# A fused encoder layer on one core: adaLN pieces by contraction tile, the output projection's end by column blocks, gate rows in pass 0

## What is computed

```
mod = c @ ada_w + ada_b                       # 2048 -> 6*2048
sh1, sc1, gt1, sh2, sc2, gt2 = split(mod, 6)
h = modulate(rmsnorm(x, norm1_g), sh1, sc1)
u = h @ w_in                                  # branches and gate pre-activations
merged = sum over 4 branches of sigmoid(gate) * y
x = x + gt1 * (merged @ w_o)                  # x1
h2 = modulate(rmsnorm(x, norm2_g), sh2, sc2)
# router: top group of 4, then the top 2 of 8 experts in it
x = x + gt2 * hier_moe(h2, ...)               # 32 SwiGLU experts, width 512
return rmsnorm(x, final_g)
```

## Time and profile before

| | us |
|---|---|
| median of 3 runs | 1788.24 |
| lowest and highest run | 1787.34, 1788.6 |
| profiled execution, span from first to last instruction | 1788.8 |

### The profile page before, as it was taken

One profiled execution on the slowest core, in us unless ns is written; L12 is line 12 of the kernel. 1 busy time (PEld: TensorE's weight loads), 2 busy tenths in 40 slices (PEclk: granted clock), 3 DMA queues, 4 the chain that ended last, 5 costly groups with the idle time before them and its releaser, 6 DMA issues.

```text
span 1788.8 us, 25899 instructions
## 1 busy us (share of the span) xinstructions
PE 1740.1 (97%) x10197; PEld 992.0 (55%) x10198; DVE 898.3 (50%) x1041; ACT 389.4 (22%) x472; POOL 0.8 (0%) x5
## 2 busy tenths in 40 slices
PE   4999999999999999999999999999999999999997
PEld 3888567777777776875444444444444444444432
DVE  5564968867778678566232323233333333333334
ACT  3001034333333333443111101010101010101011
POOL 0000000000000000000000000000000000000000
PEclk9999999999999999999999999999999999999999
DMA  9998538889879697646999999999999999999996
GB/s 370 387 374 327 188 142 336 330 312 353 332 287 363 250 373 306 227 164 246 422 422 422 422 422 422 422 421 422 421 422 422 422 422 422 422 421 422 422 422 253
DMA packets 137455, 641.95 MB, mean 359 GB/s; under 512 B 9027, under 2 KB 9155, under 8 KB 77123
## 3 DMA queue, kind: packets, MB, share of 16 engines
q1 hardware_dynamic: 136978, 639.18, 89.4%
q0 software_dynamic: 144, 1.70, 0.2%
q10 hardware_dynamic: 290, 0.46, 0.1%
HBM read 639.21 MB, written 2.10 MB: 359 GB/s over the span
## 4 chain that ended last, share of the span: by engine, by line
PE 75%; DMA 21%; DVE 2%; SPq 1%; issue 1%; ACT 0%; DVEq 0%
DMA ring<-in_exp_w 18%; PE ps L920 18%; PE ps L884 7%; PE ps L675 7%; PE ps L677 7%; PE ps L676 7%; PE ps L580 6%; PE ps L637 5%; PE ps L907 4%; PE ps L862 3%; PE ps L593 3%; DMA ring<-in_ada_w 2%; PE ps L748 2%; PE ps L749 2%; PE ps L750 2%; DVE r_m L1322 1%
## 5 line engine op out<-in xcount | busy, mean ns | idle before, releaser
L920 PE MATMUL ps<-ring 128*64 128x512 f32 x2048 | 466.7, 598 | 5.7 <-DMA ring<-in_exp_w 5.7
L920 PEld LDWEIGHTS ps<-ring 128*64 128x64 f32 x2048 | 143.4, 137 | 293.3 <-issue 293.2
L1690 DVE TENSOR_TENSOR r_h<-r_h,ps 128x1024 f32<-128x1024 f32 x124 | 145.9, 1218 | 205.2 <-PE ps L907 205.2
L676 PE MATMUL ps<-g_lo,h_hi 128*128 128x512 f32 x512 | 199.3, 389 | 0.0
L1663 DVE TENSOR_TENSOR r_c<-ps,scale 128x512 f32<-128x512 f32 x64 | 44.0, 687 | 283.9 <-PE ps L862 280.8
L1234 ACT ACTIVATE r_m<-ps 128x512 f32<-128x512 f32 x32 | 19.1, 597 | 699.3 <-PE ps L920 699.3
L675 PE MATMUL ps<-mix_hi,h_hi 128*128 128x512 f32 x384 | 156.6, 408 | 0.0
L1107 ACT ACTIVATE mix_hi<-ring 128x1024 fp32r<-128x1024 f32 x96 | 101.5, 1061 | 222.4 <-PE ps L677 222.4
L677 PE MATMUL ps<-mix_hi,h_lo 128*128 128x512 f32 x384 | 149.7, 390 | 0.0
L580 PE MATMUL ps<-r_h,ring 128*128 128x256 f32 x640 | 142.3, 385 | 1.3 <-ACT r_h L1058 1.3
L1414 DVE SCALAR_TENSOR_TENSOR r_m<-ring,col,r_m 128x2048 f32<-128x2048 f32 x53 | 124.3, 2346 | 31.4 <-DMA ring<-in_ada_w 31.4
(11 more groups left out here) (270 smaller groups left out, 1619.2 us busy)
## 6 DMA issues: line engine op xcount, KB each, us to landing
ring<-in_exp_w SPq DMA_DIRECT2D x320, 1024.0 KB, 20.2
ring<-in_ada_w SPq DMA_DIRECT2D x78, 1024.0 KB, 8.2
ring<-in_w_in SPq DMA_DIRECT2D x36, 2048.0 KB, 10.0
r_b<-in_exp_w SPq DMA_DIRECT2D x64, 1024.0 KB, 22.2
ring<-in_w_in SPq DMA_DIRECT2D x20, 1024.0 KB, 14.2
r_b<-in_ada_w SPq DMA_DIRECT2D x18, 1024.0 KB, 9.7
ring<-in_w_o SPq DMA_DIRECT2D x8, 2048.0 KB, 9.6
ring<-in_branch_w SPq DMA_DIRECT2D x6, 2048.0 KB, 8.4
```

What stands on the lines that cost most here:

```text
L676: mm(ps[:, b + t, :], h, lo[:, cols], start=False, stop=False)
L920: last = mm(ps[m * NWIN:(m + 1) * NWIN, 2, :], xe[:, k, :], chunk(2 * c + m)[:, kk * F:(kk + 1) * F], start=(k == 0), stop=(k == KT - 1))
L1690: V.tensor_tensor(x1n, x1n, ps[:, (6, 4)[b]:(6, 4)[b] + 2, :].rearrange("p b n -> p (b n)"), ALU.add).then_inc(added, 1)
```

## The change

Three places are touched.

1. In the head, the last piece of each part is loaded as four transfers of 512 KB, one for each contraction tile with shift and scale together, each with a semaphore of its own, and VectorE waits for each tile. The two saves of part 0 (units 3 and 4) go from VectorE to ScalarE.
2. At the end of the output projection the loops are turned: column block n outside, token half t inside. Pieces 30 and 29 change places on ScalarE and VectorE, so that the columns of blocks 0 and 1 need pieces 28 and 30 alone. x1, transposes, copies and logits also go by n, then t. Transposed blocks of t = 0 are copied by VectorE, those of t = 1 by ScalarE. The reciprocals of both roots are one instruction; the diagonals `root_diag` are made by ScalarE.
3. The matmuls for the gt2 rows leave the stretch between the first gathers and stand in pass 0 behind the first quarter of `first`; ScalarE saves the rows there.

```diff
+                if piece == 3:
+                    for kk in range(4):
+                        sp.dma_start(head_ada(i)[:, kk, :, :],
+                                     ada_v[:, 12 + kk, 0:2 * D].rearrange("p (v n) -> p v n", v=2)
+                                     [:, :, part * PART:(part + 1) * PART]).then_inc(ada_last[kk], 16)
+                    return
...
-            pe.wait_ge(g_lo_done, 128 + 32)
-            for t in range(TT):
-                for n in range(4):
+            for n in range(4):
+                pe.wait_ge(g_lo_done, 128 + (30 if n < 2 else 32))
+                for t in range(TT):
                     for k in (14, 15):
                         last = wo_products(k, t, n)
                     last.then_inc(wo_done, 1)
...
+            for n in range(4):
+                for t in range(TT):
+                    turn_x1(n, t)
+                if n == 1:
+                    pe.wait_ge(rw_scaled, 1)
+                if n:
+                    for t in range(TT):
+                        logit_part(n - 1, t)
...
+                    if not with_second and c == 0:
+                        gate2_row()
...
+                if k == 3:
+                    for n in (3, 4):
+                        act.wait_ge(head_used, used(0, n))
+                        A(late[:, n - 3, :], ps[:, 6:8, :].rearrange("p b n -> p (b n)"), ACT.Copy
+                          ).then_inc(part_added, 1)
...
-            for y in range(AHEAD + 1, 32):
+            for y in (*range(AHEAD + 1, 29), 30, 29, 31):
                 wo_high(y)
...
             A(stat[:, 20:21], keep[:, K_EPS:K_EPS + 1], ACT.Sqrt).then_inc(warm_up, 1)
+            copy_turned(0)
             square(0, 0)
+            copy_turned(1)
+            square(1, 0)
+            copy_turned(2)
             square(0, 1)
             root(0)
-            square(1, 0)
-            part_high(0)
+            copy_turned(3)
             square(1, 1)
             root(1)
+            part_high(0)
             part_high(1)
...
+            for n in range(4):
+                save_x1(n, 0)
+                if n:
+                    save_turned(n - 1)
+                save_x1(n, 1)
+            save_turned(3)
```

More of the change, by code:

```diff
@@ L178, in used, with ada_count @@
             return HEAD * part + ORDER[part].index(n) + 1
+        def ada_count(i):
+            return 32 * sum(j % ADA_FIRST == i % ADA_FIRST and j % 4 != 3 for j in range(i + 1))
         def head_w(i):
@@ L213, in build @@
         ada_in = [sem(f"ada_in{i}") for i in range(ADA_FIRST)]
+        ada_last = [sem(f"ada_last{i}") for i in range(4)]
         part_added = sem("part_added")
@@ L784, in _, with turn_x1, logit_part @@
                     last.then_inc(wo_done, 1)
-            for m in range(8):
-                t, n = m // 4, m % 4
-                pe.wait_ge(x1_ready, m + 1)
+            def turn_x1(n, t):
+                pe.wait_ge(x1_ready, 2 * n + t + 1)
                 for k in range(4):
-                    last = nc.tensor.transpose(ps[:, m, k * P:(k + 1) * P],
+                    last = nc.tensor.transpose(ps[:, 4 * t + n, k * P:(k + 1) * P],
                                                x1_k[:, t, n, k, :], ident)
                 last.then_inc(x1_turned, 1)
[L795 to L801, removed]
+            def logit_part(n, t):
+                pe.wait_ge((x1T_ready, x1T_copied)[t], n + 1)
                 for k in range(4 * n, 4 * n + 4):
                     side = k % 2
-                    last = mm(ps[side * NWIN:(side + 1) * NWIN, t, 0:P], rws[:, k, :], x1T[:, k, t * P:(t + 1) * P],
+                    last = mm(ps[side * NWIN:(side + 1) * NWIN, 4 * t, 0:P], rws[:, k, :], x1T[:, k, t * P:(t + 1) * P],
                               start=(k < 2), stop=(k >= KT - 2))
@@ L807, in _ @@
                     last.then_inc(logitT_done, 1)
+            for n in range(4):
[6 more added lines that the diff above has]
+                        logit_part(n - 1, t)
+            mm(ps[:, 5, 0:36], ones, cst_k[:, :], start=True, stop=False)
+            mm(ps[:, 5, 0:36], ones[0:1, :], lrow[0:1, :], start=False, stop=True).then_inc(cst_done, 1)
+            for t in range(TT):
+                logit_part(3, t)
             def logits(t):
@@ L909, in combine, with gate2_row @@
                 last.then_inc(comb_done, 1)
+            def gate2_row():
+                pe.wait_ge(diag2_ready, 1)
+                for b in range(2):
+                    for side in range(2):
+                        o = 4 * (2 * b + side)
+                        last = mm(ps[side * NWIN:(side + 1) * NWIN, 6 + b, :], ones[:, 0:NWIN], diag2[:, o:o + 4, :],
+                                  start=True, stop=True)
+                last.then_inc(gt2_row, 1)
             def first(p, with_second, last_pass=False):
@@ L957, in _ @@
             gather_parts((0, 1))
[L958 to L965, removed]
             pe.wait_ge(lo_ready, 8)
@@ L1525, in _ @@
                             mod[:, GT2, :].unsqueeze(2).broadcast_to([P, KT, P]), ALU.mult).then_inc(diag2_ready, 1)
-            for y in range(24, 32):
+            for y in (*range(24, 29), 30, 29, 31):
                 wo_low(y)
             step(V.tensor_scalar(minus, ident, -1.0, None, ALU.mult))
[L1530 to L1534, removed]
@@ L1536, in _ @@
             v.wait_ge(x_again, 16)
             v.wait_ge(row_saved, 2)
[L1538 to L1552, removed]
+            def save_x1(n, t):
+                v.wait_ge(wo_done, 2 * n + t + 1)
+                prod = slot(5)[:, t * MIX:(t + 1) * MIX]
+                step(V.tensor_tensor(prod, ps[:, 4 * t + n, :], gt1row[:, n * MIX:(n + 1) * MIX], ALU.mult))
+                x1n = x1[:, t, n * MIX:(n + 1) * MIX]
+                V.tensor_tensor(x1n, x1n, prod, ALU.add).then_inc(x1_ready, 1)
```

58 lines of the change are left out of this document (34 added, 24 removed).

## The result

| | before | after |
|---|---|---|
| median, us | 1787.47 (20 runs) | 1789.91 (20 runs) |
| lowest, highest | 1785.42, 1789.99 | 1787.29, 1793.67 |

The ratio is 1.0015, its 95% interval 1.0009 to 1.0021: the change costs 2.4 us (1.6 to 3.8). The forecast was a gain of 1.0. The profiled execution after has a time of 1790.77 and a span of 1789.0. A run's time lies 1.8 above its span, so the span of before, 1788.8, belongs to a run of some 1790.6, 3.1 above the median of its kernel and above the highest of its twenty runs. The two profiled spans are 0.2 apart where the medians are 2.4 apart, and the first thing to find is why.

What follows compares the result with a forecast made beforehand. The prediction took the expert-weight stream, started by TensorE's first release, as the bound, with TensorE ahead of it. Terms −1.4 − 0.65 + 0 + 0.75 + 0.3 = −1.0 us gave 1787.2 us, 8-in-10 range 1785.0 to 1790.2.

Steps and rivals of the forecast that it cites:

- −0.2 up to the gather: Router to first gather: later remainders (+1.7) and removed gt2 rows (−1.9) sum to −0.2 us, taken as 0.
- −1.4: Head: copy leaves VectorE's chain in part 1, a small wait leaves part 0; 1.4 us gained.
- −0.65: Head, behind part 1's sums: shorter quiet stretch, even chance that the clock stays up; half of 1.3 us gained.
- +1.7: Start of the remainders: ScalarE's scaled copy begins only behind roots, reciprocal and a diagonal; 1.7 us later.
- +0.75: Between last logits and remainders: quiet 2.5 us, even chance of a clock fall costing 1.5 us.
- −1.9: First gathers: gt2 rows fall out of TensorE's work there, 1.9 us of issue saved.
- +0.3: Pass 0: gt2 rows free later weight chunks 1.9 us later, nearly all covered by slack; 0.3 us lost.
- The 4.1 us: Projection's end: last product 4.1 us earlier without the idling and half clock, given back at once by VectorE's wait.
- The end moves as S moves: Expert-weight stream: never stops after S, its first load issue at 836.65 us; the remaining 952.15 us are its own.
- no slack in the stream: Rival, pass 0: gt2 rows cost the stream their full 1.9 us, giving 1788.8 us; chance 0.12.
- faster: Rival, projection's end: the 4.1 us reach the stream, giving 1783.1 us; chance 0.08.
- the 1.2 GHz through all remainders: Slower rival: TensorE's clock falls and stays low up to the first gather, +7.5 us, 1794.0 us; chance 0.06.

Runs made afterwards that it cites:

- e1: Head part of the change alone (last adaLN piece by contraction tile, part 0 saves on ScalarE), against the kernel before: 1785.95 us, ratio 0.9994.
- e4: Head and projection parts together, gt2 rows left between the first gathers, against the kernel before: 1789.32 us, ratio 1.0013.
- e3: Only the gt2 rows moved out of the gathers into pass 0, against the kernel before: 1787.87 us, ratio 1.0008.
- e2: Projection part alone (x1, transposes and logits by column blocks), gt2 rows left between the gathers, against the kernel before: 1792.31 us, ratio 1.0027.
- e12: e11 plus two unused matmuls in the head, ahead of and behind the sums of part 0: 1784.41 us, ratio to before 0.9983.
- e11: e10 plus two unused 256-column matmuls in TensorE's wait ahead of pass 0's first gather: 1785.01 us, ratio to before 0.9985.
- e7: Changed kernel with each pair of x1 blocks transposed behind the products of the next column block: 1787.07 us, ratio to before 0.9999.
- e8: e4 plus seven unused matmuls in TensorE's wait ahead of the remainders, mis-sized at 6.22 us: 1793.48 us, ratio to before 1.0037.
- e5: Changed kernel with the high bf16 parts made in blocks of 512 columns: 1789.26 us, ratio to before 1.0014.
- e6: Changed kernel with the gt2 rows moved from pass 0 into TensorE's wait ahead of the remainders: 1787.92 us, ratio to before 1.0007.
- e10: e7 and e6 together, early transposes and gt2 rows ahead of the remainders: 1785.27 us, ratio to before 0.9992.
- e9: e7 and e5 together, early transposes and high parts in blocks: 1785.63 us, ratio to before 0.9993.

## Why the prediction was wrong, by its steps

The runs give each part of the change a price, to be held against the terms of the prediction (which add up to −1.2 here, since the prediction took its −0.2 up to the gather as 0):

| part | forecast, us | runs, us |
|---|---|---|
| head: e1 less before | −1.4 − 0.65 = −2.05 | −1.2 |
| projection's end to the remainders, with the clock there: e4 less e1 | +1.7 + 0.75 = +2.45 | +3.4 |
| gt2 rows: after less e4 | −1.9 + 0.3 = −1.6 | +0.6 |
| sum | −1.2 | +2.8 |

After and e4 ran on different chips, so their difference is rough. Still the gt2 rows hold the largest miss: a gain was forecast and none came. e3, the rows alone, has +0.75 (interval −0.2 to +3.0), which excludes −1.6.

**1. Head, −1.4 and −0.65: too large, read from one execution.** Copy and wait are gone in after. But the wait of 1.67 us and the fall behind it belong to the one execution that was read, not to the kernel. e2 and e3 have the head of before, with the copy. TensorE lost more to a fall of the clock in part 0 there (0.62 and 0.66 granted from 36 to 45 us, against 0.81 in before), asked later, and waited 0.41 us and not at all; e3:

```profile
74.00 1.95 PE L554 MATMUL ps<-keep,r_m 128*128 128x1 f32 x16
...
76.00:80.00 4.00, 4.00 (x20) 3.51 (x20) 0.33 (x2) 2.07 (x4) 0.00 (x0) 1.00 1.06 387
```

So the clock stayed up behind part 1 without the edit, and e12, with it, has half clock there. The sums of part 2 begin at 110.46 and 110.43 in e2 and e3, and at 109.66 to 110.01 in the eight executions of e4 to e11, which have the new head and a like clock in part 0: 0.4 to 0.8 us is what the edit gave. After and e1 fell further in part 0 (0.53) and stand at 111.44 and 111.34. So the head of before's execution was some 1.8 late, as far as these two tell, and that of after some 1.4 late against the eight, which nearly cancels. That the edit gains is likely (e1 −1.2, with an interval that holds zero; e4 3.0 below e2, whose intervals meet); its size is open. Nor does every microsecond of the head arrive: of the 0.9 by which e1's sums come earlier than those of before, 0.6 is left at the projection's end. The prediction had no term for the fall in part 0.

**2. Projection's end: right in mechanism.** The 4.1 us came, and VectorE's 4.80 us of waiting gave them back; with e7's order 3.3 of them arrive at the remainders. Relative to the last logits the remainders come 1.8 later (forecast 1.7), and the router is 0.2 late, together the +2.0 of e2. The balance of −0.2 up to the gather was not reached, since with the gt2 rows out TensorE waits 0.45 us there for VectorE.

**The clock, +0.75: half of its price, and in another place.** A coin between 0 and 1.5 was taken, for the wait ahead of the remainders. Of the profiled executions with this wait of 1.71, e2, e4 and e7 had the fall behind it and after had not (granted 1.00 from 813.21 to 826.50). That, and not the rows of 1.92 and 2.56 us, which are of two lengths, shows the same stretch falling on either side. The fall is worth 1.65 in e4 against e8. After fell at the gathers instead, where the dense gt2 rows had stood, and this was not priced at all: its sixteen matmuls took 5.02 us for 3.5, and from `first` to S lie 5.21 us against 4.18 before, so 1.0 reached S. That this is near the 0.75 is luck. The clock fell at the gathers in after, e5, e6 and e10, and not in e3, e7 and e9, which lack the rows too; with rows (before, e1, e2, e4, e8) or filler (e11, e12) it never did. That the rows held it is thus likely, and not shown. The Trainium skill, page "TensorE: Matmul & The Clock Gate", section "HAM oscillation — how this bites in real kernels", tells of a kernel in which waits between bursts of matmuls bring the array back to its slow clock, so that the next burst starts slow. The rows of after and of e10 agree in kind, behind waits of about 0.45 us.

**3. gt2 rows in pass 0, +0.3: the step that failed.** "The end moves as S moves" took S as the release that binds, and the slack was worked out for the second and third pair alone. The fifth pair is released by TensorE too, behind the gt2 rows, the rest of pass 0 and the first quarter of pass 1. Before, it was issued 3.6 us ahead of its need; 3.0 later, with a stream that had begun 1.1 later and lost 0.5, it had 2.2, too little by 1.3. That this pair bound is shown for this execution. How much later than S the stream ends, against before, tells what the rows cost it:

| execution | later behind S, us |
|---|---|
| rows in pass 0: after, e3, e5, e7, e9 | **+1.4**, **+1.7**, +0.3, +0.7, +0.5 |
| rows elsewhere: e1, e2, e4, e6, e8, e10, e11, e12 | 0.0, +0.1, +0.1, −0.1, 0.0, −0.3, 0.0, −0.5 |

The two groups do not meet: the rows in pass 0 cost the stream something each time. How much varies, and why is open. In after, e5, e7 and e9 a hole stands some 22 us behind S, at the fifth pair; e3 loses its share ahead of that. The rival "no slack in the stream" had 1.9. So most of the −1.9 in step 2 was no gain: rows taken out of the gathers and put ahead of the later releases still delay these. The latency was too kind as well: 1.6 us from issue to bytes, taken from a start; what a stream that runs dry needs is more. The windows of after have 57 GB/s from 0.3 to 1.3 us behind the issue at 837.72, half the rate up to 2.3 us, and full rate only from there on. The Trainium skill, page "DMA: Bandwidth & Descriptors", section "Specifications", gives about 0.6 us to the first byte for loads issued by SP; the first of these windows agrees, and of the time to full rate, which decides here, the figure says nothing.

Put together from the two profiled executions: −0.8 at the sums of part 2, +0.8 from there to `first`, +1.0 from `first` to S, +1.4 behind S, +2.5 in all (rounded terms). These add up by construction, and each is of one execution. Of the rivals "no slack" came true in good part; "faster" was there to be had only with another order of TensorE's list and the rows elsewhere (e11); the 1.2 GHz through all remainders did not come.

Two slips are in the prediction's frame. The median was taken as 0.6 below the execution that was read; time against time it lies 2.4 below, and the median of twenty runs 3.1. And the terms named for the upper end of the range give 1788.24 + 0.4 + 0.5 + 1.6 = 1790.7, not 1790.2. Neither moves the forecast.

Open: how often each fall of the clock happens. The profiles show one execution each. The median of e2 (+5.2, against 3.4 for e4 less e1) may hold more of them, or a larger gain of the head.

## What to carry to other kernels

Where a fixed stream follows, ask of every load in it, not of the first, how long ahead of its need it is issued; work moved behind the first release still delays the later ones. A gain ahead of an engine that is last next shows only once that engine's order is changed with it: here transposes between the products. Before a wait is priced, see in a second execution whether it is there: the 1.67 us of the head were not. And work that leaves a sparse stretch may cost more than it weighs, if it was what kept the clock up; here that is likely, and not shown.

## What the hardware showed unexpectedly

The granted clock goes with the time of a run. In the changed kernel the three runs at 0.996 or 0.997 took 1787.3 to 1787.7, the five at 0.993 1790.4 to 1793.7; much of the spread between runs goes with it.

The gt2 rows, whose matmuls alternate between the two halves of the output's partitions, take 1.94 us for eight, 0.24 each. The fourteen of e8's filler, same shape, all into one half, took 6.22, 0.44 each, at a granted clock of 1.00. They also all write one and the same bank, so whether the half or the bank makes the difference is not shown.
